# Projection and decode attention of a hybrid decoder step as one stage: keys turned in 32x32 blocks by VectorE, scores over four key quarters at once, one convolution operation per tap

## The chip, the cores and the metric

The kernel runs on one core of one Trainium2 chip. The metric is the device time of one execution in microseconds (us), as the median of several. "GB/s" is what the core's 16 DMA engines moved. PE is TensorE, PEld its weight load, DVE is VectorE, ACT is ScalarE, POOL is GpSimd, SP is SyncE, which here only issues DMAs.

## What is computed

One inference step with one layer: 256 prompt tokens and 8 sequences of 4 new tokens (32 decode tokens, 288 in all), model width 1024, all float32. Each token goes through a mixer with two head groups and then through a mixture of 32 experts. What matters here is the input projection, the short convolution of head group A, and the decode part of head group B, whose 8 sequences have 1024 past keys and values each, in pages of 128 rows that a page table scatters over a pool:

```python
proj = h @ w_in
qkv_g, z_g, beta_in, a_in, qkv_s = jnp.split(proj, [c1, c2, c3, c4], axis=-1)
conv_out, conv_new = causal_short_conv(qkv_g, conv_buf, conv_w)      # width 4, then SiLU
...
past_k = cache_k[l][page_table].reshape(bs, -1, SB_HEADS, HEAD_DIM)  # 8 heads x 64
z = jnp.einsum('bqhd,bkhd->bhqk', q_blk, k) * scale + bias_f
mask = key_pos[None, :] < pos[:, None]
log_rem = jnp.where(mask, jax.nn.log_sigmoid(-z), 0.0)
after = lax.cumsum(log_rem, axis=3, reverse=True) - log_rem
a = jnp.where(mask, jnp.exp(jax.nn.log_sigmoid(z) + after), 0.0)
out = jnp.einsum('bhqk,bkhd->bqhd', a.astype(v.dtype), v)
```

So each weight of a key is sigmoid(z) times the product of (1 - sigmoid(z)) over all later keys. Head group A (a delta rule in chunks of 64) and the experts follow; the change hardly touches them.

## The kernel before

The program is written by hand: each engine has its own list of instructions, in blocks, and semaphores (`wait_ge`, `then_inc`) tie the engines together. Every engine executes its list strictly in order. At the end of a block all engines meet. A ring of 12 slots of 1 MB (`ring`, `slot(u)`) holds whatever is loaded: the projection's weights in 7 column groups of 2 MB, then the cache pages, then `w_out`, and later the experts' chunks.

**Block 1, projection.** `tiles` is the order of the 29 output tiles of 128 columns: 12 `conv`, `ba`, 4 `z`, 4 `q`, 4 `k`, 4 `v`. For each tile PE does 8 matmuls of 128x128 by 128x288 (L410), ACT copies the result out, DVE does the convolution (`conv`, eight operations for each tile, L627 to L631: four taps, each once for the prompt and once for the decode tokens) and the multiplication by the sigmoid (`silu`, L639). After the next tile PE turns what must lie token by token (`turn`).

**Block 2, decode attention.** 16 steps (`STEPS`), each with one page of keys of 4 sequences. In a step PE turns the 16 key blocks by matmuls with the identity (`turn_keys`, L824), ACT and DVE copy half of them each out of PSUM (L947, L993), and PE forms the scores (`scores`, L836), with sequences side by side in four groups of 32 PE columns. For each half of 512 keys ACT makes two sigmoids (`betas`, L915), DVE a running product and a multiplication (`past_weights`, L973, L975), PE turns the weights (`turn_A`, L848), and `values` (L859) sums the value pages, which lie in the ring as loaded. `own_heads` (L872) picks each head's own columns. Pages are loaded by `load_cache`, one page at a time: a `value_load` of the page's number (L206) and then the DMA (L207), from SP and from GpSimd.

Then come block 3 (prompt part of head group B and first products of group A, up to 265.8 us), the rest of group A, `w_out`, the router and, from about 376 us on, the experts in 16 pairs. Their weights stream from HBM through the same ring (L761).

Of the kernel before, what the change touches and what calls it, by code (L numbers as in the profile page):

```python
# [13 lines left out]
ALU = mybir.AluOpType  # L14
# [7 lines left out]
NH = 8  # L22
# [38 lines left out]
def build(nc, x_prompt, x_sample, cache_k, cache_v, page_table, state_conv, state_ssm, norm_mix, w_in, conv_w,  # L61
# [4 lines left out]
    with ctx:  # L66
# [10 lines left out]
        X = sb("X", [P, 3, D])  # L77
        wb = sb("wb", [P, D])
# [42 lines left out]
        E = const(2, P)  # L121
        Sel = const(2, 16)
        headmask = const(512)
        sel8, hch = const(P), const(512)
# [12 lines left out]
        vs_tok, zg = at(A1, (3, GW)), at(A1 + 3 * GW, (HP, T))  # L137
# [6 lines left out]
        s_small, s_small2 = sem("conv_state_loaded"), sem("small_loaded")  # L144
# [5 lines left out]
        s_ringfree = sem("ring_used")  # L150
# [6 lines left out]
        s_ax, s_ex, s_qbd = sem("abs_a"), sem("log1p_a"), sem("query_blocks")  # L157
# [5 lines left out]
        GROUP_COL = [0, GW, 2 * GW, C_Z, C_S, C_S + GW, C_S + 2 * GW]  # L163
# [7 lines left out]
        s_gpage = [sem(f"pages_loaded_by_gpsimd{i}") for i in range(4)]  # L171
# [4 lines left out]
        def slot_count(u):  # L176

            return sum(16 * (PGL if U_C <= v < U_WO else 1) for v in range(u % NSLOT, u + 1, NSLOT)
                       if (U_C <= v < U_WO and v - U_C not in BY_POOL) or (not U_C <= v < U_WO and v % 2 == 0))

        def slot_wait(eng, u):
            m = u - U_C
            if U_C <= u < U_WO and m in BY_POOL:
                return eng.wait_ge(s_gpage[m % 8 // 2], PGL * 16 * ((m - 11) // 8 + 1))
            return eng.wait_ge(slot_sem(u), slot_count(u))

        def slot_free(eng, u, n):

            if u + n > NSLOT:
                eng.wait_ge(s_ringfree, u + n - NSLOT)  # L190

        def load_w_in(eng, n):
            slot_free(eng, 2 * n, 2)
            eng.dma_start(slot(2 * n, 2).rearrange("p (k n) -> p k n", k=KD),
                          w_in_v[:, :, GROUP_COL[n]:GROUP_COL[n] + GW]).then_inc(slot_sem(2 * n), 16)

        CACHE_UNITS = [("k", 0, 1), ("k", 0, 0), ("v", 0, 1), ("k", 1, 1), ("v", 0, 0), ("k", 1, 0), ("v", 1, 1), ("v", 1, 0)]

        def load_cache(eng, m):

            (what, g, ph), pg = CACHE_UNITS[m // 4], m % 4
            kv = "kv".index(what)
            slot_free(eng, U_C + m, 1)
            for s in range(4):
                col = NPG * (4 * g + s) + PGL * ph + pg
                page = eng.value_load(pt[0:1, col:col + 1], min_val=0, max_val=POOL - 1)  # L206
                eng.dma_start(slot(U_C + m)[:, s * GW:(s + 1) * GW],  # L207
                              (cache_k, cache_v)[kv][0, bass.ds(page, 1)].rearrange("o p h d -> (o p) (h d)"))\
                   .then_inc(s_gpage[m % 8 // 2] if m in BY_POOL else slot_sem(U_C + m), 16)
# [7 lines left out]
        class Norm:  # L217


            def __init__(self, nth, rowbuf, weight_wait, turned, ready=lambda e: None, inner=1):  # L220
                self.order = lambda v: v.rearrange("p (q k) -> p k q", k=inner)
                self.dest = lambda v: v.rearrange("p (k q) -> p k q", k=inner)
                self.rowbuf, self.weight_wait, self.turned, self.ready = rowbuf, weight_wait, turned, ready
                self.base = 3 * nth

            def scalar(self, act):
                self.ready(act)
                for t in range(3):
                    r = rows(t)
                    act.activation(self.rowbuf(t), X[r, t, :], ACT.Square, accum_out=stat[r, t, 0:1]).then_inc(s_nsq, 1)  # L230
                for t in range(3):
                    r = rows(t)
                    act.wait_ge(s_nsq, self.base + t + 1)
                    act.activation(stat[r, t, 1:2], stat[r, t, 0:1], ACT.Sqrt, scale=1.0 / D,
                                   bias=epst[r, 0:1]).then_inc(s_nstd, 1)
                if self.turned:
                    for t in range(3):
                        act.wait_ge(s_ntp, self.base + t + 1)
                        b = 2 * (t % 2)
                        n = ROWS[t]  # L240
                        act.activation(hT[:, :, toks(t)],
                                       bank[:, b:b + 2, :].rearrange("p b n -> p (b n)")[:, 0:KD * n]
                                       .rearrange("p (k n) -> p k n", k=KD), ACT.Copy).then_inc(s_nev, 1)

            def vector(self, dve):
                c = Chain(dve, s_dve)
                c.n = dve_n[0]
                self.weight_wait(dve)
                for t in range(3):
                    r = rows(t)  # L250
                    dve.wait_ge(s_nstd, self.base + t + 1)
                    c(dve.reciprocal(stat[r, t, 2:3], stat[r, t, 1:2]))
                    dve.scalar_tensor_tensor(out=self.dest(self.rowbuf(t)), in0=self.order(X[r, t, :]), scalar=stat[r, t, 2:3],
                                             in1=self.order(wb[r, :]), op0=ALU.mult, op1=ALU.mult).then_inc(s_nrow, 1)
                dve_n[0] = c.n

            def tensor(self, pe):
                for t in range(3):
                    pe.wait_ge(s_nrow, self.base + t + 1)
                    if t == 2:  # L260
                        pe.wait_ge(s_nev, self.base + 1)
                    b, n = 2 * (t % 2), ROWS[t]
                    dst = bank[:, b:b + 2, :].rearrange("p b n -> p (b n)")
                    for k in range(KD):
                        ins = pe.transpose(dst[:, k * n:(k + 1) * n], self.rowbuf(t)[:, k * P:(k + 1) * P],
                                           ident[0:n, 0:n])
                    ins.then_inc(s_ntp, 1)


        hrow = lambda t: work[rows(t), A2 + D * t:A2 + D * (t + 1)]  # L270
        s_id, s_t = sem("identity_ready"), sem("turned")

        B0 = A2
        pad = [work[:, B0 + 316 * i:B0 + 316 * i + 315] for i in range(2)]
        B1 = B0 + 632
        turnT = [work[:, B1 + T * i:B1 + T * (i + 1)] for i in range(2)]
        B2 = B1 + 2 * T
        csig = work[:, B2:B2 + 2 * T].rearrange("p (b n) -> p b n", b=2)
        B3 = B2 + 2 * T

        cdec, cpro = work[0:NSEQ * 7, B3:B3 + CONVD], work[64:67, B3:B3 + CONVD]
        kst = at(B3 + CONVD, (3, GW))
# [2154 lines left out]
```

## Time and profile before

| | |
|---|---|
| time, median of 3 | 1309.69 us (1308.79 to 1310.25) |
| span of the profiled execution | 1313.2 us, 20103 instructions |
| profiled execution against the median | 3.5 us above it |
| PE, DVE, ACT, POOL busy | 1253.0, 402.9, 247.9, 97.3 us |
| moved | 463.64 MB, mean 353 GB/s |

The page names no other time for the profiled execution than its span, first to last instruction. A stretch of one stage is read from the windows and from the time line, not from the shares over the whole span.

### The profile page before, as it was taken

The numbers are of one execution on the slowest core, as the hardware profiler recorded it, in microseconds if no ns is written. First come the engines' busy times: TensorE is split into PE (matmuls) and PEld (weight loads), VectorE is DVE, ScalarE is ACT, GpSimd is POOL, SyncE is SP. The second block draws the span as 40 slices with busy tenths as digits, with TensorE's granted clock in tenths as the row PEclk, the third lists the DMA queues.
The fourth block names the chain that finished last, engine by engine and source line by source line (L and its number), as shares of the span: only waits on it lengthen the run. The fifth ranks groups of instructions, "written<-read, shape, count | busy, mean of one in ns | idle before, by whom it ended". The sixth has DMA issues, their size and how long they took to land.

```text
span 1313.2 us, 20103 instructions
## 1 busy us (share of the span) xinstructions
PE 1253.0 (95%) x7924; PEld 566.2 (43%) x7924; DVE 402.9 (31%) x912; ACT 247.9 (19%) x416; POOL 97.3 (7%) x172
## 2 busy tenths in 40 slices
PE   8999998989999999999999999999999999999996
PEld 6777775687443333333333333333333333333332
DVE  4721343642742222322222232222213322212323
ACT  3223332623211110110111011011101101011103
POOL 6101142252000000000000000000000000000000
PEclk9999998999989999999999999999999999999999
DMA  9643699020799999999999999999999999999994
GB/s 319 237 128 92 226 373 339 9 88 7 280 334 382 425 428 429 426 429 428 428 430 425 429 428 424 431 428 429 425 430 429 426 430 426 430 427 427 429 427 185
DMA packets 68156, 463.64 MB, mean 353 GB/s; under 512 B 16910, under 2 KB 17038, under 8 KB 41478
## 3 DMA queue, kind: packets, MB, share of 16 engines
q1 hardware_dynamic: 64536, 451.17, 83.9%
q0 software_dynamic: 3520, 11.54, 2.4%
q8 instruction: 38, 0.62, 0.2%
q10 hardware_dynamic: 46, 0.18, 0.0%
q14 instruction: 16, 0.13, 0.0%
HBM read 459.15 MB, written 3.70 MB: 352 GB/s over the span
## 4 chain that ended last, share of the span: by engine, by line
PE 55%; DMA 23%; issue 1%; ACT 1%; DVE 0%; SPq 0%; DVEq 0%; ACTq 0%
PE bank L2130 25%; DMA ring<-in_w_up 20%; PE bank L2163 6%; PE bank L2099 4%; PE bank L2078 4%; PE bank L2143 3%; PE bank L1588 2%; DMA ring<-in_w_down 2%; PE bank L2082 1%; PE bank L2103 1%; PE bank L1453 1%; PE bank L1443 1%; PE bank L1450 1%; PE bank L2190 1%; PE bank L2119 0%
## 5 line engine op out<-in xcount | busy, mean ns | idle before, releaser
L2130 PE MATMUL bank<-ring,work 128*64 128x512 f32 x1280 | 288.5, 604 | 19.4 <-DMA ring<-in_w_up 19.4
L2130 PEld LDWEIGHTS bank<-ring,work 128*64 128x64 f32 x1280 | 91.7, 139 | 213.5 <-issue 202.9
L2163 PE MATMUL bank<-ring,work 128*64 128x512 f32 x768 | 172.3, 596 | 7.7 <-ACT work L2265 5.3
L410 PE MATMUL bank<-hoT,ring 128*128 128x288 f32 x448 | 115.1, 412 | 0.8 <-ACT hoT L445 0.5
L2163 PEld LDWEIGHTS bank<-ring,work 128*64 128x64 f32 x768 | 54.8, 137 | 103.4 <-issue 98.7
L410 PEld LDWEIGHTS bank<-hoT,ring 128*128 128x128 f32 x448 | 84.9, 193 | 23.7 <-issue 0.7
L2364 DVE TENSOR_SCALAR work<-bank 128x512 f32<-128x512 f32 x32 | 22.1, 690 | 231.5 <-PE bank L2143 230.5
L2249 ACT ACTIVATE work<-bank 128x1024 f32<-128x1024 f32 x16 | 16.4, 1024 | 385.9 <-PE bank L2082 365.1
L2323 DVE TENSOR_TENSOR X<-X,bank 128x512 f32<-128x512 f32 x64 | 44.0, 688 | 120.7 <-PE bank L2099 120.7
L2377 DVE COPY work<-bank 128x512 f32<-128x512 f32 x16 | 11.1, 692 | 211.5 <-PE bank L2163 211.5
L2099 PE MATMUL bank<-work 128*128 128x512 f32 x128 | 59.2, 605 | 0.0
L2143 PE MATMUL bank<-ring,work 128*64 128x512 f32 x256 | 56.3, 592 | 1.5 <-DMA ring<-in_w_up 1.5
L2130 PE MATMUL bank<-work 128*64 128x512 f32 x128 | 56.6, 595 | 0.0
L2130 PE MATMUL bank<-hoT,work 128*64 128x512 f32 x128 | 56.6, 595 | 0.0
L2143 PE MATMUL bank<-work 128*64 128x512 f32 x128 | 56.2, 592 | 0.0
L2163 PE MATMUL bank<-hoT,work 128*64 128x512 f32 x128 | 56.2, 592 | 0.0
L2143 PE MATMUL bank<-hoT,work 128*64 128x512 f32 x128 | 56.2, 592 | 0.0
L2163 PE MATMUL bank<-work 128*64 128x512 f32 x128 | 56.2, 592 | 0.0
L2078 PE MATMUL bank<-gq,work 128*128 128x512 f32 x120 | 54.0, 592 | 0.0
L2261 ACT ACTIVATE work<-work 128x512 f32<-128x512 f32 x32 | 20.1, 627 | 144.5 <-DVE work L2364 144.5
L2369 DVE TENSOR_TENSOR work<-work 128x512 f32<-128x512 f32 x32 | 38.9, 1215 | 18.8 <-ACT work L2261 16.6
L2265 ACT ACTIVATE work<-bank 128x512 f32<-128x512 f32 x32 | 19.1, 597 | 111.4 <-PE bank L2171 111.4
(414 smaller groups left out, 1396.2 us busy)
## 6 DMA issues: line engine op xcount, KB each, us to landing
ring<-in_w_up SPq DMA_DIRECT2D x96, 2048.0 KB, 24.7
ring<-in_w_down SPq DMA_DIRECT2D x48, 2048.0 KB, 26.6
work<-in_w_up SPq DMA_DIRECT2D x16, 2048.0 KB, 24.2
hoT<-in_w_up SPq DMA_DIRECT2D x16, 2048.0 KB, 28.6
work<-in_w_down SPq DMA_DIRECT2D x16, 1024.0 KB, 22.7
hoT<-in_w_down SPq DMA_DIRECT2D x16, 1024.0 KB, 24.6
ring<-in_w_in SPq DMA_DIRECT2D x7, 2048.0 KB, 16.0
ring<-in_cache_k SPq DMA_DIRECT2D x48, 256.0 KB, 3.0
```

Source lines behind the costliest of these rows:

```text
L410: ins = pe.matmul(bank[0:m, i % 2, 0:T], w[:, k, :], hT[:, k, :], start=k == 0, stop=k == KD - 1)
L1588: ins = pe.matmul(bank[q, WO_BANK[t, m], :], oT[:, k, toks(t)], w[:, k, :], start=k >= HP if t == 2 else k == HP, stop=k < HP if t == 2 el ...
L2078: pe.matmul(bank[:, 6 + m, :], Pm[:, t * P:(t + 1) * P], h2[:, t, 512 * m:512 * (m + 1)], start=t == 0, stop=False)
L2099: pe.matmul(bank[:, 4 + n, :], PGT[:, t * P:(t + 1) * P], oo[:, 512 * m:512 * (m + 1)], start=True, stop=True).then_inc(M["y"], 1)
L2130: ins = pe.matmul(bank[CAP * e:CAP * e + CAP, g, :], xT[:, k, CAP * e:CAP * e + CAP], weight(odd, ch + e, k % 2 * RSLOT + 512 * g), start= ...
L2143: ins = pe.matmul(bank[CAP * e:CAP * e + CAP, g, :], xT[:, k, CAP * e:CAP * e + CAP], weight(odd, 6 + e, k % 2 * RSLOT + 512 * g), start=F ...
L2163: ins = pe.matmul(bank[CAP * e:CAP * e + CAP, 4 + m, :], aT[:, k, CAP * e:CAP * e + CAP], weight(odd, ch + e, k % 4 * D + 512 * m), start= ...
L2261: act.activation(sg, gb, ACT.Sigmoid, scale=1.702).then_inc(M["sigmoid"], 1)
L2265: act.activation(aT[:, 4 * half:4 * half + 4, :].rearrange("p k s -> p (k s)"), bank[:, half, :], ACT.Copy)\
L2323: dve.tensor_tensor(x, x, bank[:, 4 + n, :], ALU.add).then_inc(M["y_added"], 1)
L2364: dve.tensor_scalar(gb, hu[:, :, 0], 7.0, None, ALU.min).then_inc(M["gate_clamped"], 1)
L2369: dve.tensor_tensor(ab[:, 512 * half:512 * (half + 1)].rearrange("p (k q) -> p k q", k=4), by_k(ub), by_k(sg), ALU.mult).then_inc(M["act"], 1)
```

## The change

Blocks 1 and 2 become one block. The attention's projections come first (`q`, `k`, `v`, `ba`, then `conv` and `z`), and pieces of the decode attention stand between the tiles on each engine's list. Nearly everything is loaded in 25 pairs of slots (`PAIRS`), 2 MB each, by SP alone, in the written order; pair n waits until pair n-6 has been used up. A pair of keys or values is now all 8 pages of one sequence. A page of keys goes to 32 partitions, four rows of the page side by side, so that eight pages fill the tile; VectorE turns it in place in 32x32 blocks (two instructions of 128x2048), after which one matmul contracts 32 dimensions of 4 key groups (a quarter of the keys each) at once with a block-diagonal query matrix `Q32`. `Q32` lies over `X` and `wb`, so x is loaded again later. The running product goes over 256 keys per group, and small operations join the four groups. The convolution runs over prompt and decode tokens in one operation per tap; GpSimd does the SiLU multiplication and the squares, VectorE the normalisation that GpSimd did. The gate of `z` moves into block 3 (one ACT and one DVE operation over 128x1152).

```diff
-        U_C, U_WO, U_END = 14, 46, 50
-        PGL = 4
-        BY_POOL = [m for m in range(11, 32) if m % 2]
+        PAIRS = [("w", "q"), ("K", 0), ("K", 1), ("w", "k"), ("K", 2), ("K", 3), ("w", "v"), ("V", 0), ("V", 1), ("K", 4), ("K", 5),
+                 ("w", "c0"), ("V", 2), ("V", 3), ("w", "c1"), ("K", 6), ("K", 7), ("w", "c2"), ("V", 4), ("V", 5), ("w", "z"),
+                 ("V", 6), ("V", 7), ("o", 0), ("o", 1)]
...
-            for s in range(4):
-                col = NPG * (4 * g + s) + PGL * ph + pg
-                page = eng.value_load(pt[0:1, col:col + 1], min_val=0, max_val=POOL - 1)
-                eng.dma_start(slot(U_C + m)[:, s * GW:(s + 1) * GW],
...
+                def used(q):
+
+                    what, n = PAIRS[q]
+                    if what == "w":
+                        sp.wait_ge(s_pj, group_end(n) + 1)
+                    elif what == "K":
+                        sp.wait_ge(s_sc, n + 1)
+                    else:
+                        sp.wait_ge(s_av, n + 1)
+
+                def load_pair(q):
+                    what, n = PAIRS[q]
+                    if what in "KV":
+                        order = KEY_PAGES if what == "K" else range(NPG)
+                        pages = [sp.value_load(pt[0:1, NPG * n + pg:NPG * n + pg + 1], min_val=0, max_val=POOL - 1) for pg in order]
+                    if q >= NPR:
+                        used(q - NPR)
...
+                    elif what == "K":
+                        for pg, page in zip(order, pages):
+                            kb, odd = pg // 2, pg % 2
+                            sp.dma_start(tile[32 * kb:32 * kb + 32, 4 * GW * odd:4 * GW * (odd + 1)].rearrange("p (q c) -> p q c", q=4),
...
+                load_x()
+                sp.dma_start(pt, page_table.rearrange("(o s) n -> o (s n)", o=1)).then_inc(s_pt, 16)
+                load_pair(0)
+                sp.wait_ge(s_pt, 16)
+                for q in range(1, len(PAIRS)):
+                    load_pair(q)
...
+                    for s in (2 * b, 2 * b + 1):
+                        pe.wait_ge(s_kt, s + 1)
+                        keys = pair_tile("K", s).rearrange("p (g c) -> p g c", g=8)
+                        for m in range(4):
+                            for j in range(HP):
+                                cb = 4 * j + m
+                                ins = pe.matmul(bank[32 * j:32 * j + 32, 6, 256 * (s % 2):256 * (s % 2) + 256]
...
+                    if i == 19:
+                        turn_A(2)
+                        own_heads(1)
+                        scores(3)
...
+                    if i == 22:
+                        turn_A(3)
+                        own_heads(2)
+                    if i == 24:
+                        values(3)
+                        square_sums(range(3))
+                    if i == 25:
+                        square_sums(range(3, 5))
...
+                def turn_keys(s):
+
+                    pair_wait(dve, "K", s)
+                    for h in range(2):
+                        v = pair_tile("K", s)[:, 2 * PAST * h:2 * PAST * (h + 1)]
+                        ins = dve.transpose(out=v, in_=v)
+                    ins.then_inc(s_kt, 1)
...
+                    if i == 18:
+                        own(1)
+                        turn_keys(6)
+                    if i == 19:
+                        turn_keys(7)
+                    if i == 21:
+                        own(2)
+                        weights(3)
```

**How the lists stand now, at three places.** SP, where the first cached keys are loaded. Before (`ring<-in_cache_k` is a page of keys into the ring, `TENSOR_LOAD` with its `ISA` rows the reading of one page number):

```order
L206 TENSOR_LOAD work [waits ring_used,small_loaded]
L206 ISA x2
L207 ISA
L207 DMA ring<-in_cache_k 128x512
L206 TENSOR_LOAD work
L206 ISA x2
L207 ISA
L207 DMA ring<-in_cache_k 128x512
```

Of the change, the last page number of the pair and the first pages of V0, the first pair that waits for the scores:

```order
L298 TENSOR_LOAD work
L298 ISA x2
L314 ISA [waits scores_done]
L314 DMA ring<-in_cache_v 128x512
L314 ISA
L314 DMA ring<-in_cache_v 128x512
```

A pair's eight page numbers are now read ahead of the pair's wait and its eight DMAs; they are as many as before for each page, and all of them are SP's.

VectorE, where the last two sequences' keys are turned (of the change; L916 and L918 are the convolution's taps, L906 is the multiplication by the head mask, L837 the turning):

```order
L916 TENSOR_SCALAR work<-work 128x312 [waits conv_silu,projection_copied]
L918 SCALAR_TENSOR_TENSOR work<-work 128x312 [waits dve_chain] x3
L906 TENSOR_TENSOR work<-bank,work 128x512 [waits heads_turned,values_summed]
L837 STREAM_TRANSPOSE ring<-ring 128x2048 [waits slot_loaded4]
L837 STREAM_TRANSPOSE ring<-ring 128x2048
L916 TENSOR_SCALAR work<-work 128x312 [waits conv_silu,projection_copied]
L918 SCALAR_TENSOR_TENSOR work<-work 128x312 [waits dve_chain] x3
L837 STREAM_TRANSPOSE ring<-ring 128x2048 [waits slot_loaded6]
L837 STREAM_TRANSPOSE ring<-ring 128x2048
```

Between the two pairs of turnings now stands one whole tile's convolution, and ahead of the first another one and the mask.

TensorE, near the end of the stage (of the change; L503 is a projection tile, L464 and L471 the values, L491 the sums of squares):

```order
L464 MATMUL bank<-work 32x512 [waits slot_loaded4,slot_loaded6,own_heads,A_copied]
L464 MATMUL bank<-work 32x512
L471 MATMUL bank<-ring,work 32x512 x16
L491 MATMUL bank<-work 128x288 [waits convstate_copied,squares]
L491 MATMUL bank<-work 128x288 [waits squares] x2
L503 MATMUL bank<-hoT,ring 128x288 [waits slot_loaded2,projection_copied]
L503 MATMUL bank<-hoT,ring 128x288 x7
L387 MATMUL bank<-ident,work 59x128 [waits convstate_copied,projection_copied]
L491 MATMUL bank<-work 128x288 [waits logs_and_roots,squares] x2
```

Before, the sums of squares stood between the `k` tiles, and the logarithms that the fourth one waits for (`logs_and_roots`, on ACT) were made tile by tile beside them; now the first logarithm stands on ACT's list behind the copy of tile 25.

## Rows read from the trace of the kernel before

**Rows 1.** Windows by stage: busy time of each engine, granted clock, DMA share, GB/s

```profile
0.00:145.80 145.80, 137.87 (x594) 101.99 (x595) 54.68 (x168) 39.71 (x105) 32.62 (x98) 1.00 0.58 188
145.80:220.20 74.40, 68.54 (x1014) 49.98 (x1014) 29.70 (x35) 25.66 (x33) 23.85 (x44) 1.00 0.99 359
376.00:1313.00 937.00, 898.86 (x4140) 311.28 (x4138) 240.26 (x527) 127.13 (x178) 0.00 (x0) 0.99 0.98 415
```

**Rows 2.** The chain that ended last, in time: start, us, what

```profile
681.01 7.07 PE bank L2130 x32
688.81 26.68 DMA ring<-in_w_up
...
748.76 25.49 DMA ring<-in_w_up
```

**Rows 3.** Time line of PE in block 1: start, us, what

```profile
14.96 10.13 PE L410 MATMUL bank<-hoT,ring 128*128 128x288 f32 x32 [0.47 <-ACT hoT L445]
...
130.66 0.49 PE L387 MATMUL bank<-ident,work 128*128 128x128 f32 x3
130.99 4.05 PE L410 MATMUL bank<-hoT,ring 128*128 128x288 f32 x16
134.87 0.49 PE L387 MATMUL bank<-ident,work 128*128 128x128 f32 x3
```

**Rows 4.** Time line of PE in block 2 and at its end

```profile
149.56 2.08 PE L824 MATMUL bank<-ident,ring 128*128 128x128 f32 x16 [0.33 <-ACT hoT L947]
151.57 1.08 PE L836 MATMUL bank<-hoT,work 128*32 128x128 f32 x32
...
173.43 3.62 PE L859 MATMUL bank<-ring,hoT 128*32 128x512 f32 x32
...
202.62 1.07 PE L872 MATMUL bank<-work,wb 128*128 128x16 f32 x8
...
212.10 1.92 PE L859 MATMUL bank<-ring,hoT 128*32 128x512 f32 x16 [3.31 <-DMA ring<-in_cache_v]
...
220.24 0.82 PE L1130 MATMUL bank<-work 64*64 64x65 f32 x16 [0.57 <-PEq L793]
```

**Rows 5.** Time line of SP, DMA issues: start, us, what

```profile
2.35 1.25 SPq L194 DMA_DIRECT2D ring<-in_w_in  x2
3.65 6.53 SPq L319 DMA_DIRECT2D work<-in_sb_bias  x1
...
13.93 0.38 SPq L326 DMA_DIRECT2D wba<-in_w_in  x1
...
126.95 8.06 SPq L207 DMA_DIRECT2D ring<-in_cache_v  x8
```

**Rows 6.** Lines L206 and L207 on SP: duration ns min/median/max, landing times

```profile
L206 SPq TENSOR_LOAD <-work x84: 262/268/851, 50.2 to 200.4; - x84
L207 SPq DMA_DIRECT2D ring<-in_cache_k x32: 333/338/388, 51.2 to 114.9; - x32
DMA to landing us min/median/max: 2.5/2.9/3.8
```

**Rows 7.** Windows 182 to 200 us: only cache pages are being loaded

```profile
182.00:200.00 18.00, 18.00 (x275) 13.06 (x268) 8.16 (x10) 5.89 (x8) 8.04 (x15) 1.00 1.04 388
```

**Rows 8.** DVE groups by shape up to 220 us: busy us, mean ns | idle before

```profile
L630 DVE SCALAR_TENSOR_TENSOR gq<-work,gq 128x256 f32<-128x256 f32 x36 | 17.4, 485 | 1.3
L993 DVE COPY work<-bank 128x1024 f32<-128x1024 f32 x8 | 9.8, 1224 | 20.4 <-PE bank L824 20.4
L973 DVE TENSOR_TENSOR_SCAN work<-work 128x512 f32<-128x512 f32 x4 | 5.1, 1282 | 3.2 <-ACT work L916 3.1
L675 DVE MEMSET work<- 128x1024 f32 x1 | 0.9, 912 | 0.2 <-issue 0.2
```

**Rows 9.** ACT groups by shape up to 220 us

```profile
L463 ACT ACTIVATE hoT<-bank,epst 128x288 f32<-128x288 f32 x8 | 3.8, 497 | 0.8 <-PE bank L423 0.6
L457 ACT ACT_TABLE_LOAD x1 | 1.3, 1283 | 0.0
```

**Rows 10.** Windows around two falls of the granted clock (the column before the DMA share)

```profile
218.00:220.00 2.00, 1.06 (x8) 0.97 (x8) 0.54 (x1) 0.22 (x1) 0.00 (x0) 1.00 1.05 383
222.00:230.00 8.00, 8.00 (x49) 4.88 (x45) 2.53 (x3) 2.97 (x4) 0.83 (x2) 0.50 0.85 186
270.00:274.00 4.00, 2.22 (x76) 2.13 (x72) 0.69 (x1) 1.20 (x3) 4.00 (x3) 1.00 0.99 417
274.00:278.00 4.00, 3.81 (x89) 3.81 (x90) 1.69 (x3) 0.00 (x0) 0.15 (x1) 0.66 0.17 54
```

**Rows 11.** Time line at the end of block 3

```profile
264.65 0.83 DVE L1285 TENSOR_TENSOR ring<-ring,work 128x256 f32<-128x256 f32 x1
```

More of the change, by code:

```diff
@@ L215, in build @@
             sem(f"norm_{n}") for n in ("squares", "std", "rows", "turned", "copied"))
[L217 to L267, printed above, removed]
@@ L270, in build @@
         hrow = lambda t: work[rows(t), A2 + D * t:A2 + D * (t + 1)]
         s_id, s_t = sem("identity_ready"), sem("turned")
+        PADW, CW = 316, 312
         B0 = A2
[L274 to L281, printed above, removed]
@@ L282, in build @@
[L282 to L286 removed]
+        pad = [work[:, B0 + PADW * i:B0 + PADW * i + 315] for i in range(2)]
+        B1 = B0 + 2 * PADW
+        cbuf = [work[:, B1 + CW * i:B1 + CW * (i + 1)] for i in range(2)]
+        B2 = B1 + 2 * CW
+        csig = [work[:, B2 + CW * i:B2 + CW * (i + 1)] for i in range(2)]
+        B3 = B2 + 2 * CW
+        NCS = 3 + 7 * NSEQ
@@ L287, in build @@
+        cst = work[0:NCS, B3:B3 + CONVD]
+        B4 = B3 + CONVD
+        baT = work[0:2 * NH, B4:B4 + TP]
+        B5 = B4 + TP
+        turnT = [work[:, B5 + T * i:B5 + T * (i + 1)] for i in range(2)]
+        kst = at(B5 + 2 * T, (3, GW))
+        l2 = at(B5, (KD, T))
+        B6 = B5 + 2 * T + 3 * GW + 192
+        assert KD * T <= 2 * T + 3 * GW + 192
         gq = sb("gq", [P, 12, TP])
-        baT = work[0:2 * NH, B3 + 2 * CONVD:B3 + 2 * CONVD + TP]
-        tiles = [("conv", j) for j in range(12)] + [("ba", 0)] + [("z", j) for j in range(4)] + \
-                [("q", j) for j in range(4)] + [("k", j) for j in range(4)] + [("v", j) for j in range(4)]
@@ L291, in build @@
-        I_BA, I_Q, I_SS = 12, 17, 18
+        tiles = [("q", j) for j in range(4)] + [("k", j) for j in range(4)] + [("v", j) for j in range(4)] + [("ba", 0)] + \
+                [("conv", j) for j in range(12)] + [("z", j) for j in range(4)]
+        I_K, I_BA, I_C, I_Z = 4, 12, 13, 25
         turned_tiles = [i for i, (kind, _) in enumerate(tiles) if kind in ("k", "v", "ba")]
@@ new lines, in build @@
+        AT = work[:, ZG:ZG + 512]
+        om = work[:, ZG + 2 * T:ZG + 2 * T + 512]
+        incl = work[:, B6:B6 + 514].rearrange("p (s c) -> p s c", s=2)
+        B7 = B6 + 514
+        AnT = work[0:ND, B7:B7 + NH * ND]
+        B8 = B7 + NH * ND
+        seg, segT, aft, aftT = (work[:, B8 + 32 * i:B8 + 32 * i + 32] for i in range(4))
+        B9 = B8 + 128
+        Tnew, carry, im16, Sel2, d4 = work[:, B9:B9 + 8], work[:, B9 + 8:B9 + 10], work[:, B9 + 10:B9 + 26], \
+            work[:, B9 + 26:B9 + 34], work[:, B9 + 34:B9 + 38]
@@ L448, in _, with query_blocks @@
                 c = Chain(act, s_act)
-                m = 0
+                def query_blocks(a):
+                    act.wait_ge(s_q32, 1)
+                    act.wait_ge(s_pje, 4)
+                    for db in range(2):
+                        r = HD * a + 32 * db
+                        src = qsT[r:r + 32, :, SEQ:T].rearrange("p h (s i) -> p h s i", i=NDEC)
+                        for kb in range(4):
+                            dst = Q32[32 * kb:32 * kb + 32].rearrange("p s (h a d) n -> p h a d s n", h=HP, a=2)
+                            ins = act.activation(dst[:, :, a, db, :, 16 * a + 4 * kb:16 * a + 4 * kb + 4], src, ACT.Copy)
+                    return ins
@@ L730, in _ @@
+                    if i == 21:
+                        own(2)
+                        weights(3)
+                    if i == 25:
+                        own(3)
+                        log_gates()
+                for n in range(4):
+                    dve.wait_ge(s_rt, 8 + n + 1)
+                    dve.tensor_tensor(gq[:, 2 * n:2 * n + 2, 0:T], gq[:, 2 * n:2 * n + 2, 0:T], l2[:, 2 * n:2 * n + 2, :], ALU.mult)
                 dve_n[0] = c.n
@@ L1230, in _ @@
                 betas(1)
+                act.activation(zs, zg, ACT.Sigmoid).then_inc(s_zs, 1)
                 copy_kv(0)
```

862 lines of the change are left out of this document (431 added, 431 removed).

## The prediction

> **What bounds the kernel now.** I read the windows by stage first. Up to 145.8 us PE is busy 137.9 of 145.8 us and DMA 0.58 of the time: the projection is bound by PE. From 145.8 to 220.2 PE has 68.5 of 74.4 us and DMA 0.99: both are nearly full, and PE's work there contains the turning of the keys. From 376 us on DMA has 0.98 at 415 GB/s and PE 899 of 937 us [rows 1]. The chain of waits tells which of these two sets the end: from 681 us on it goes through the landing of `w_up`, with 25.5 to 26.7 us at a step [rows 2]. The experts are a stream that begins when the mixer ends, so I take the end to move one to one with the moment when block 3 begins, now 220.24 us [rows 4]. DVE, ACT and POOL are far from full everywhere. The whole question is thus: when does PE finish the new stage?
>
> **PE's own work.** A tile took 134.87 - 130.99 = 3.88 us to the row behind it, and three turns put 130.99 - 130.66 = 0.33 ahead of it [rows 3]. 29 x 3.88 = 112.5; 8 `k`/`v` turns 2.6; `ba` and 12 conv turns 1.8; masks 0.8; 8 sums of squares of 288 columns, each an eighth of a tile, 3.9. Scores: an old step's 32 matmuls of 128 columns take 1.0 to 1.1 us with four groups side by side [rows 4]; now a sequence has 16 matmuls of 256 columns, again four side by side, which I put at 1.85, and 8 x 1.85 = 14.8. Values: 3.6 us for 32 of 512 columns [rows 4], now a little more for two sequences with the new tokens, 4.5; x 4 = 18. Turning of weights and `own_heads`, 1.0 each [rows 4], x 4 = 8; new tokens 0.8. Sum 163.2. PE begins at 14.96 [rows 3], so alone it would end at 178.2. What is gone is 16 times 2 us of key turning [rows 4] and the waits at the end of block 2, such as 3.31 us [rows 4]; that is the promise, 42 us.
>
> **SP.** Eight page issues take 8.06 us, so a page costs (8.06 - 0.34)/7 = 1.10 us of SP, number and DMA together [rows 5, 6]. I split it into 0.64 for the number, which now stands ahead of the pair's wait, and 0.46 for the DMA. 16 pairs are 141 us of one queue that GpSimd used to share. A pair needs 8.8 us of SP but 2.1 MB / 388 GB/s = 5.4 us of transfer [rows 7]. SP, not the bytes, paces the pages. From the page table's landing near 8.8 us: K0 to 17.7, seven small DMAs (0.4 to 0.6 each [rows 5]) to 21.8, K1 to 30.6, then `w` for `k`, which lands 5.4 + 2.9 [rows 6] + 0.7 (K1's last page) later, 40.1. K2, K3 to 48.6; `w` for `v` lands 58.1. V0 waits in SP's order for the scores of sequence 0 (54); V0, V1, K4, K5 go out to 85; `w` for c0 lands 94.0. V3 waits for the first values (107); c1 lands 119.8, just in time.
>
> **PE's waits by this time line.** (1) First `k` tile: ready at 14.96 + 4 x 3.88 + 0.8 = 31.3, weights at 40.1: 8.8 us. (2) First conv tile: ready at 86.9, weights 94.0: 7.1. (3) Scores of sequences 6 and 7. DVE does them in order: mask, two turnings, a convolution, two turnings. The ring's turning has no row. Nearest rows, per element of a partition: MEMSET 912/1024 = 0.89 ns, COPY 1.2, SCAN 2.5 [rows 8]; so 1.8 to 5.1 us for 2048. I take 2.2, near the copy, since it also reads and writes once; 4.4 a sequence. The four convolution operations over 312 columns are 4 x about 0.56 us, from 485 ns for 256 [rows 8]. The keys are then 2.0 and 4.8 us late: 6.8. (4) `turn_A(3)` waits for a convolution, the mask and `weights(3)`: 4.0. (5) The fourth sum of squares waits for the first logarithm, which stands behind ACT's copy of tile 25, a sigmoid, and two table loads of 1.28 us [rows 9]: 4.9. Sum 31.6 us, so PE ends at 209.8; copy, two last logarithms, one table load, four exponentials and DVE's product make block 3 begin at 212.7, against 220.2: -7.5.
>
> **What the rows don't price.** *Key pages into 32 partitions.* Every page row is of 128 partitions. Lower bound: their rate, 388 GB/s, 5.4 us a pair. Upper bound: half of it, 10.8 us, if a quarter of the partitions takes only half of the engines' rate. Up to 8.8 it mostly hides behind SP's issuing. At 10.8 K0 to K3 push `w` for `k` and `v` back: my sum over the time line gives +20, at 9.4 +10.7, at 7.5 +4.2. I take 7.5, since pages for four partition groups are in flight together: +4.2. The Trainium skill, "SBUF — State Buffer", section "Door 1: The DMA port swizzle", has 32 partitions reach 8 of 16 ports (189 GB/s where all reach 328), and "Can I just issue two DMAs to hit both halves?" says that two transfers to both halves gain little; by it the term would be the one at 10.8 and the sum 1329, and no row of before shows such a transfer.
>
> *The clock.* Where PE had idled half of 208.8 to 220.2, the granted clock fell from full to 0.50 (1.2 GHz) for 222 to 230, and about 2 us of idle at 272 gave 0.66 over the next four [rows 10]. Half of 3.4 us is 1.7; of 10 us, 5. Three shorter waits at 1.7 and two longer at 2.6 make 10; part is absorbed where PE waits for DVE or ACT next: +8. Bounds 0 and 15.
>
> *The gate in block 3.* DVE is last there, to 265.48 [rows 11], and gets one operation over 128x1152, 1.2 ns each [rows 8]: +1.3; ACT's stays under PE. *Entry of block 3*: it ran 8 us at half clock [rows 10]; the new stage's tail idles less: -2.5 of 4.
>
> **At nothing**, with their cover: DVE's convolution (12 x 2.3, less than before) and POOL's SiLU and square (under 2 us a tile of 3.88); the query blocks, 16 small ACT operations, under PE's tiles; POOL's clearing of 128x4096 (3.6 us by rows 8 on DVE, perhaps twice that on POOL) under 16 us of `q` tiles; loading x again, 1.2 MB, late in the stage, where DMA has room (0.58 in block 1 [rows 1]). With the cover gone each costs 1 to 4 us. ACT's copies stay under 1 us a tile: 497 ns is an activation of 288 [rows 9].
>
> **Sum:** -7.5 + 4.2 + 8 + 1.3 - 2.5 = +3.5 us. The profiled execution's span is 1313.2, 3.5 above the median of 1309.7; so the span becomes 1316.7 and the median 1313.2.
>
> **Rivals.** 0.2% is 2.6 us, about what this kernel's measurement can tell from no change.
> (a) *Faster by a few us*: pages land at full rate and PE's waits stay too short or too well absorbed to lower the clock. -7.5 + 0 + 2 + 1.3 - 2.5 = -6.7, 1303; down to 1296 if the first `k` tile's wait (8.8) goes too, by a cheaper page on SP. For: DMA has slack outside K0 to K3. Against: the two falls of the clock [rows 10]. 0.26.
> (b) *PE-bound as in block 1*: SP's page costs less when numbers are read back to back, turning is 1.8 us. PE ends near 185, block 3 begins near 188, 32 us earlier: 1309.7 - 32 + 1.3 = 1279. Against: 1.10 us on SP for each page [rows 5]. 0.06.
> (c) *Nothing measurable*: the terms above cancel; 1307 to 1312. 0.17.
> (d) *Slightly slower, my forecast*: 1312.3 to 1319. 0.25.
> (e) *Key pages at half rate*: 9.4 us a pair instead of 7.5 adds 10.7 - 4.2 = 6.5, 10.8 adds 16; near the middle +9 beyond the forecast, 1322, and 1329 at the end. It decides above about 9 us a pair, where transfer passes SP's 8.8. 0.18.
> (f) *DVE's turnings at the scan's price*, 2 x 5.1 us a sequence instead of 4.4: wait (3) grows by 5.8 for each of two sequences, less some 2 that the other waits then save, and K2 to K5 delay the `turned` copies behind them: +9.5, 1323. For: a 32x32 turning isn't a streaming copy. Against: only the upper row says so. 0.08.
>
> **From these:** faster 0.26 + 0.06 = 0.32, same 0.17, slower 0.51. The losses hold most, and the working gives 1313; the range of (d) alone is 1312 to 1319. The range has to hold (a), (c), (d), and most of (e) and (f): 1296 to 1327, which leaves out (b) and the far ends.
>
> **What the profile of after would show.** Block 3 begins at about 225 (212.7 + 4.2 + 8), against 220.24. SP: 8.8 us per page pair, no idle between K0 and K3. The first `k` tile begins near 40, the first conv tile near 96, each after idle of over 6 us, then granted clock 0.5 for some us. A STREAM_TRANSPOSE of 128x2048 takes 2.2 us. PE idles ahead of `scores(3)` and of the fourth sum of squares. The key pages' issue-to-landing tells (e): over 5 us where it was 2.9 [rows 6]. Behind each of these: if the k tile starts at 35, SP's page is cheaper (b); if DVE's turning is near 5 us, (f).
> What would make it wrong altogether: a wait that I haven't seen in the new order, since on SP, DVE and ACT every wait holds all that is queued behind it. SP's waits for V0 and V3 hold K4 and the conv weights; DVE's waits for a landing of keys hold the `turned` copies and convolutions, on which ACT's copies and PE's next tiles depend. Or the experts, if they don't follow the stage one to one: being DMA-bound they would, but a stage that ends with the first experts' weights less far ahead in the ring would give part of a gain back.

## The result and the profile after

The changed kernel takes 1331.26 us (median of 4, 1329.68 to 1331.52) against 1309.97 for the kernel before, measured beside it (1308.79 to 1313.65): the medians are 21.3 us apart, and the ratio over all their executions is 1.0153, 95% interval 1.0137 to 1.0169. It is slower by 1.5%; the prediction was 1313 us, range 1296 to 1327. The profiled execution has a span of 1329.8 us.

Block 3 begins at 244.9 us, 25 us later than before; the prediction had 225, 5 us later, and 42 us earlier was the promise if TensorE never waited. In what follows K0 and V0 are the keys and values of sequence 0, and c0, c1, c2 and z the column groups of `w_in` for the conv and `z` tiles, as in `PAIRS`. TensorE's time line in the new stage, all rows ahead of which it idled for over 2 us (they answer to [rows 3, 4]):

```profile
42.80 10.99 PE L503 MATMUL bank<-hoT,ring 128*128 128x288 f32 x32 [9.51 <-DMA ring<-in_w_in]
105.36 6.56 PE L503 MATMUL bank<-hoT,ring 128*128 128x288 f32 x16 [12.26 <-DMA ring<-in_w_in]
139.41 6.60 PE L503 MATMUL bank<-hoT,ring 128*128 128x288 f32 x16 [4.75 <-DMA ring<-in_w_in]
163.48 1.93 PE L439 MATMUL bank<-ring,Xw 128*32 128x256 f32 x32 [2.95 <-DVE ring L837]
169.81 3.64 PE L439 MATMUL bank<-ring,Xw 128*32 128x256 f32 x32 [4.39 <-DVE ring L837]
195.64 2.07 PE L449 MATMUL bank<-ident,hoT 128*128 128x128 f32 x8 [4.42 <-DVE hoT L898]
223.97 2.26 PE L491 MATMUL bank<-work 128*128 128x288 f32 x4 [4.81 <-ACT work L624]
244.90 0.68 PE L1165 MATMUL bank<-work 64*64 64x65 f32 x16 [2.54 <-PEq L281]
```

Seven waits, 43.1 us, each where the prediction had placed one except the third (c1); the eighth row is block 3's own beginning. Behind a wait the next work is slow: the first conv tile takes 6.56 us where one takes 4.05. The windows show the two things that go with it: the granted clock, and what DMA moves while keys (84 to 92, 144 to 152), values and `v` weights (60 to 68) or c0's weights (98 to 104) come, and DMA almost idle from 109 to 121:

```profile
14.60:244.90 230.30, 184.47 (x1022) 125.55 (x1023) 98.38 (x167) 43.21 (x123) 36.85 (x101) 0.88 0.76 230
...
60.00:68.00 8.00, 8.00 (x63) 5.79 (x56) 5.12 (x4) 1.93 (x3) 0.00 (x0) 1.00 1.05 386
84.00:92.00 8.00, 8.00 (x37) 4.48 (x36) 6.06 (x15) 0.65 (x2) 0.00 (x0) 1.00 1.03 241
109.00:121.00 12.00, 12.00 (x83) 6.78 (x85) 8.11 (x15) 3.39 (x11) 0.13 (x1) 0.95 0.05 18
144.00:152.00 8.00, 8.00 (x51) 3.55 (x50) 5.53 (x14) 1.02 (x5) 2.20 (x4) 0.97 1.07 241
98.00:104.00 6.00, 0.00 (x0) 0.00 (x0) 0.00 (x0) 0.00 (x0) 0.00 (x0) 0.50 1.05 396
```

With keys the DMA engines are as busy as with values (share 1.03 to 1.07), but move 241 GB/s instead of 386. From issue to landing a page of keys took 3.0 to 13.1 us, median 6.8: the prediction's sign for rival (e), over 5 us, is there. SP's time line:

```profile
25.82 3.87 SPq L310 DMA_DIRECT2D ring<-in_cache_k  x8
29.73 0.45 SPq L303 DMA_DIRECT2D ring<-in_w_in  x1
...
60.40 13.57 SPq L314 DMA_DIRECT2D ring<-in_cache_v  x16
78.59 12.86 SPq L310 DMA_DIRECT2D ring<-in_cache_k  x16
...
92.51 0.43 SPq L303 DMA_DIRECT2D ring<-in_w_in  x1
98.24 27.41 SPq L314 DMA_DIRECT2D ring<-in_cache_v  x16
...
127.48 1.12 SPq L303 DMA_DIRECT2D ring<-in_w_in  x1
```

V0 goes out at 60.4, c0's weights at 92.5, and V3 and c1 stand in SP's queue until the first values (121) have freed V0. The turning has its price on VectorE:

```profile
L837 DVE STREAM_TRANSPOSE ring<-ring 128x2048 f32<-128x2048 f32 x16 | 36.0, 2286 | 17.7 <-DMA ring<-in_cache_k 17.7
```

### The profile page after: what moved, and what is told of

Same layout as the page of the kernel before. It is cut to its first block, busy times and chain, and to the rows that moved or that the text cites. A ratio compares the mean times of both kernels' runs of the same rounds, so it can differ in the third digit from the quotient of the medians.

```text
span 1329.8 us, 18991 instructions
## 1 busy us (share of the span) xinstructions
PE 1233.0 (93%) x7378; PEld 538.1 (40%) x7378; DVE 424.8 (32%) x887; ACT 236.1 (18%) x417; POOL 87.2 (7%) x162
## 4 chain that ended last, share of the span: by engine, by line
PE 54%; DMA 22%; issue 1%; ACT 1%; DVE 0%; SPq 0%; DVEq 0%; ACTq 0%
PE bank L2169 25%; DMA ring<-in_w_up 20%; PE bank L2202 6%; PE bank L2138 4%; PE bank L2117 4%; PE bank L2182 3%; PE bank L1626 2%; DMA ring<-in_w_down 2%; PE bank L2121 1%; PE bank L2142 1%; PE bank L1481 1%; PE bank L1491 1%; PE bank L1488 1%; PE bank L2229 1%; PE bank L2158 0%
## 5 line engine op out<-in xcount | busy, mean ns | idle before, releaser
L503 PE MATMUL bank<-hoT,ring 128*128 128x288 f32 x448 | 127.6, 446 | 27.0 <-DMA ring<-in_w_in 26.5
L503 PEld LDWEIGHTS bank<-hoT,ring 128*128 128x128 f32 x448 | 92.6, 211 | 58.3 <-issue 30.5
L2362 DVE TENSOR_TENSOR Xw<-Xw,bank 128x512 f32<-128x512 f32 x64 | 44.0, 687 | 122.1 <-PE bank L2138 122.1
L2416 DVE COPY work<-bank 128x512 f32<-128x512 f32 x16 | 11.1, 692 | 211.6 <-PE bank L2202 211.6
L837 DVE STREAM_TRANSPOSE ring<-ring 128x2048 f32<-128x2048 f32 x16 | 36.0, 2286 | 17.7 <-DMA ring<-in_cache_k 17.7
```

The costliest lines, as they stand in the source:

```text
L503: ins = pe.matmul(bank[0:m, i % 2, 0:T], w[:, k, :], hT[:, k, :], start=k == 0, stop=k == KD - 1)
L837: ins = dve.transpose(out=v, in_=v)
L2362: dve.tensor_tensor(x, x, bank[:, 4 + n, :], ALU.add).then_inc(M["y_added"], 1)
```

## The experiments

All times are medians; "before" is the kernel before measured beside each run, 1309.6 to 1311.2 us. "Less" without more is against the changed kernel's 1331.26.

**A second trace of before.**

> The kernel before once more, for a second trace of it: the profiled execution of before took 3.5 us more than the median and lost it between 266 and 377 us, if that was a matter of this execution; then this trace has a span near 1309, block 3 again begins at 220.2, and the experts begin near 373 instead of 376.9. If the stretch is always that long, the experts begin at 377 again.

Measured: span 1308.0, block 3 at 219.38 (220.24 in the first trace), the experts at 371.95 (376.91). The first trace thus held 5.0 us that belonged to its execution, 3.4 of them behind 266 us. Compared with this one, the changed kernel's block 3 begins 25.5 us later; block 3 itself is 2.5 us shorter (42.4 against 44.9), the rest up to the experts 1.1, and the experts begin 22.0 later, at 393.91: which is the difference of the medians, 21.3, within 1 us. It lies in the new stage.

**Rate and issue of the pages.** Three kernels. In the first, keys lie over 128 partitions (the scores are then those of wrongly placed keys):

```diff
-    sp.dma_start(tile[32 * kb:32 * kb + 32, 4 * GW * odd:4 * GW * (odd + 1)]..., cache_k[...]"o (q r) h d -> (o r) q (h d)"...)
+    sp.dma_start(tile[:, GW * pg:GW * (pg + 1)], cache_k[...]"o p h d -> (o p) (h d)"...)
```

> Key pages are loaded as the value pages lie, each over 128 partitions; nothing else changes (the scores are then those of wrongly placed keys; the work is the same). Rate theory: what pushed the projection's weights back is that a page into 32 partitions moves at about 250 GB/s; then a pair of keys falls from 8.4 to 5.4 us, the waits of PE ahead of the first k tile (9.5 us) and the first conv tile (12.3 us) shrink by 4 to 8 us together, and the time by 15 or more below 1331. Issue theory: SP's 8.6 us for each pair of pages sets the pace whatever the transfer takes; then the GB/s of a pair rises, the waits stay within 2 us of what they were, and the time stays at 1329 to 1331. Both at once, by my sum over the time line: 1325, 6 us less, since the queue then waits for SP.

In the second the page numbers of keys and values are constants (other pages are attended to, and a pair's eight pages lie next to each other in memory):

```diff
-    pages = [sp.value_load(pt[0:1, NPG * n + pg:NPG * n + pg + 1], ...) for pg in order]
+    pages = [NPG * n + pg for pg in order]
```

> The page numbers are constants instead of being read from the page table: SP issues the same 128 page transfers without the 0.6 us for each number (other pages are attended to; the work is the same). Issue theory: SP's pair falls from 8.6 to 3.9 us, the two long waits of PE shrink by over 10 us together, the time to 1310 or less. Rate theory: keys still move at 250 GB/s, 8.4 us a pair, so the weights behind them come at most by the first pages' head start earlier, 4 us, and the time is 1325 or more. My sum for both at once: 1318.

> The two edits together. If rate and issue are two paces of the same stream, of which the slower sets the time, each alone brings little and both together much more than their sum: my sum gives 1300, 31 us less than 1331, against 19 for the two alone. If only one of them matters, the result is that of the one.

Measured: 1326.03, 1327.26 and 1305.94 us, so 5.2, 4.0 and 25.3 us less; the third has ratio 0.9971 (0.9955 to 0.9987) to before. Neither theory alone holds: rate and issue are two paces of one stream, and mending one leaves the other. My sums for that had 1325, 1318 and 1300: right for the first, 9 and 6 us too low for the others. The third shows what both paces are worth together, not that the kernel before was free of them: numbers at no cost relieve the values too, and before had to read its numbers as well. TensorE's waits ahead of the `k` and the first conv tile were 9.4 and 10.8 us in the first kernel, 7.6 and 7.9 in the second, and in the third:

```profile
32.68 9.69 PE L502 MATMUL bank<-hoT,ring 128*128 128x288 f32 x32 [1.24 <-DMA ring<-in_w_in]
112.12 5.65 PE L502 MATMUL bank<-hoT,ring 128*128 128x288 f32 x16 [3.25 <-DMA ring<-in_w_in]
...
215.70 0.68 PE L1164 MATMUL bank<-work 64*64 64x65 f32 x16 [2.54 <-PEq L281]
```

The wait ahead of the first conv tile is gone; the one at 112 is c1's.

**Why keys are slow.** A block ahead of the stage loads pages in eight forms and does nothing else (one execution):

> A block ahead of the stage loads 16 pages of keys of 256 KB (12 in the last form) in eight forms, one form after the other, and does nothing else, so that each form has its own stretch of some 11 us or more: (1) each page over 128 partitions, one row of 2 KB each; (2) 32 partitions with four rows each, groups in the kernel's order, neighbours far apart; (3) the same in the order of the pages; (4) as (2), every second page from ACT's queue; (5) 64 partitions from 0, two rows each; (6) 64 partitions from 32; (7) as (1) from two queues; (8) 32 partitions, always the first group. Partition theory: what counts is how many of the partitions a page covers, not the 2 KB rows, which are the same in all: forms 1 and 7 move 380 GB/s or more, 2, 3 and 8 about 250; form 6, in both halves, is well above form 5. Queue theory: pages of two queues run at once, so form 4 gets above 330. If the partitions don't matter and the changed kernel's 250 GB/s come from its pace of issue, forms 2 and 3 move 350 or more.

Windows inside the forms, in their order (the last column is GB/s):

```profile
8.00:12.00 4.00, 0.00 (x0) 0.00 (x0) 0.00 (x0) 0.00 (x0) 0.00 (x0) 1.00 1.02 387
20.00:32.00 12.00, 0.00 (x0) 0.00 (x0) 0.00 (x0) 0.00 (x0) 0.00 (x0) 1.00 1.07 236
38.00:54.00 16.00, 0.00 (x0) 0.00 (x0) 0.00 (x0) 0.00 (x0) 0.00 (x0) 1.00 1.07 213
64.00:70.00 6.00, 0.00 (x0) 0.00 (x0) 0.00 (x0) 0.00 (x0) 0.00 (x0) 1.00 1.06 352
76.00:92.00 16.00, 0.00 (x0) 0.00 (x0) 0.00 (x0) 0.00 (x0) 0.00 (x0) 1.00 1.07 200
102.00:108.00 6.00, 0.00 (x0) 0.00 (x0) 0.00 (x0) 0.00 (x0) 0.00 (x0) 1.00 0.94 337
114.00:122.00 8.00, 0.00 (x0) 0.00 (x0) 0.00 (x0) 0.00 (x0) 0.00 (x0) 1.00 1.05 394
126.00:138.00 12.00, 0.00 (x0) 0.00 (x0) 0.00 (x0) 0.00 (x0) 0.00 (x0) 1.00 1.07 201
```

The same 2 KB rows move at 387 GB/s over 128 partitions, 236 into groups of 32 that alternate between the halves, 213 in the order of the pages, 201 into one group. 64 partitions that lie in one half give 200, 64 across the middle 337. So it is the half of the partitions that is reached at one moment, not the 32. The half and the 64 that are no better than 32 agree with the Trainium skill, "SBUF — State Buffer", section "Door 1: The DMA port swizzle". Two queues, each in its own half, give 352: 49% above one queue. The same page of the Trainium skill gives, in the section "Can I just issue two DMAs to hit both halves?", two transfers to both halves 6%; for these page streams the measurement decides.

**TensorE's clock.** Matmuls that nobody reads, ahead of the seven waits:

```diff
+    for _ in range(n):
+        pe.matmul(bank[:, 2, 0:256], ident[:], hT[:, 0, 0:256], start=True, stop=True)
```

> Ahead of each of the seven long waits TensorE now does matmuls of 128x256 whose result nobody reads, each block sized a little shorter than the wait; nothing else changes. Clock theory: of the 25 us by which block 3 begins later, about 16 are work at half clock behind the waits (the k tiles, the first tile of c0 and of c1, the turning of the last weights, the last sums of squares), and a wait for a landing comes earlier when PE is earlier, since SP's order hangs on PE's progress; then the granted clock of the stage rises from 0.89 to about 0.97 and the time falls by 10 to 14, to 1317 to 1321. Rival: what runs at half clock is absorbed by the next wait, and the time stays at 1328 or more.

Measured: 1322.22, 9.0 us less; granted clock of the stage 0.99 (to 234.5 us) instead of 0.88, block 3 at 234.55. The `k` weights still land at 43.8, and two waits for weights (1.4 and 4.4 us) stay. But 9.0 is the least that the clock is worth: c0's weights landed at 104.8 (issued at 91.2, 13.6 us to landing) while the filling ran until 108.5, and c1's at 139.2 while it ran until 140.4. The filling itself so cost up to 3.6 and 1.2 us, and the clock is worth 9 to 14 us.

**Order of the loads, and places of the work.**

```diff
-  PAIRS = q K0 K1 k K2 K3 v  V0 V1 K4 K5 c0 V2 V3 c1 K6 K7 c2 V4 V5 z  V6 V7 o0 o1
+  PAIRS = q k  K0 K1 K2 v K3 V0 K4 V1 c0 K5 V2 V3 c1 K6 K7 V4 c2 V5 V6 V7 z  o0 o1
```

> Only the order of the 25 pairs on SP changes: the weights for k come ahead of the first keys, those for v and c0 each one or two pairs earlier, and z's last. Order theory: the bytes and SP's time for each pair are the same, but PE's first two long waits (9.5 and 12.3 us) and that ahead of c1 (4.8 us) go, with the half clock behind them, while the waits for DVE and ACT (22 us ahead of the last scores, the last weights and the fourth sum of squares) stay: my sum gives 23 us less, 1308. Supply theory: SP and DMA are full through the stage whatever the order, so the wait only moves to a later pair, and the time is 1325 or more.

Measured: 1323.74, 7.5 us less, a third of what I had worked out. The `k` wait is gone, but c0 is waited for 5.2 us, c1 4.2 and `v` 2.4, and 4.7 us go where TensorE waits for VectorE's copy, which stands behind the turning of K3.

```diff
-  turn_keys(6) after tile 18, turn_keys(7) after 19, weights(3) after 21 behind own(2); square_sums(3, 4) after 25, (5 to 7) after 26
+  turn_keys(6) after tile 17, turn_keys(7) after 18, weights(3) after 20;               square_sums(3, 4) after 26, (5 to 7) after 27
```

> Only the places on the lists of VectorE and TensorE change: the last two turnings of keys come one tile earlier, the last weights ahead of a convolution and of the mask, and the last five sums of squares one tile later, behind tiles 26 and 27. Place theory: the waits of 2.95, 4.39, 4.42 and 4.81 us and most of the half clock behind them go, while the waits for loads stay: my sum gives 12 us less, 1319. Rival: the same work only collides elsewhere on VectorE, whose mask for the second pair of sequences then comes later, and the time stays within 3 us of 1331.

Measured: 1323.14, 8.1 us less (12 expected); the five executions spread from 1317.9 to 1326.4. Four waits of 16.6 us in sum became three, 1.5 for the last keys, 3.2 for values and 1.5 for VectorE's mask. But in the traced execution, the slowest of the five, `k` was waited for 14.0 us and c1 6.0.

> Both edits, the order of the pairs and the places of work. If PE's waits are the whole loss, the two gains add up: 35 us less than 1331, so 1296, block 3 begins near 210, 14 us faster than the kernel before. If the supply of pages sets the stage once PE waits less, it comes out at 1305 or more, near the better of the two alone.

Measured: 1310.42, ratio 0.9996 (0.9982 to 1.0010): 20.8 us less than the changed kernel, and as fast as before, not faster. The two alone sum to 15.6; the difference is of the size of their spread. 35 was expected: in the trace the loads set a part again (waits of 4.3, 6.2 and 5.0 us for weights).

> Order and places as in the run before, and key pages over 128 partitions (the scores are of wrongly placed keys; the work is the same). Supply theory: after the order is mended, what is left of PE's waits (4.3, 6.2 and 5.0 us for weights, 2.8 for values) comes from the keys' 250 GB/s; then they go, and the time falls from 1310 by 12 or more, to 1298 or less. Issue theory: SP's page numbers hold it; then it falls by less than 5.

Measured: 1299.84, ratio 0.9920 (0.9894 to 0.9946): 10.6 us less, between the two theories. The waits for c0 (5.2) and c1 (4.2) stay; the rate is not all that makes them.

> Order and places as in the run before, and matmuls that nobody reads ahead of the three waits for weights and of the last scores. The half clock behind these waits costs some 8 us by my sum over the tiles; with the clock kept the time falls by 4 to 7 from 1310, to 1303 to 1306, and the kernel is faster than before. If the waits for loads take the gain back, it stays at 1309 or more.

Measured: 1312.78, ratio 1.0013 (0.9995 to 1.0030): a miss. In its trace TensorE waits 4.5 us for VectorE's copy (3.4 without the filling) and 4.4 for values (2.8), and block 3 begins at 222.1 where it began at 223.2: c0's weights landed at 97.3 as without the filling (97.2), c1's at 129.7 (131.2). What the filling gives back ahead of such a landing goes into the wait for it.

**Keys from two queues.** `KEY_PAGES[::2]` (partitions 0 to 63) from SP, `KEY_PAGES[1::2]` from ScalarE, two pages at a time between its copies.

> The changed kernel's order and places, and nothing left out: of each pair of keys SP issues only the four pages for the partitions 0 to 63, ScalarE's queue the four for 64 to 127 (two at a time between its copies). In the run on page forms two queues on opposite halves moved about 350 GB/s, one queue 238. If rate and issue of the key pages are the cause, both are relieved at once (6.0 instead of 8.4 us of transfer, 4.4 instead of 8.6 us of SP for a pair), and the time falls to 1308 to 1316, towards the 1306 of the run with both edits. If ScalarE's 1.1 us for each page holds its copies and with them TensorE (35 us more on its list), the gain is lost there and the time is 1325 or more.

> The same division of the key pages together with the order of pairs and the places of work of the run that had both; nothing is left out. Keys over all partitions gave 1300 there against 1310; two queues relieve SP too, so I expect 1294 to 1302, and the kernel faster than before by about 1%. If ScalarE's list becomes the wait, it stays at 1308 or more.

Measured: 1340.34, ratio 1.0208 (1.0180 to 1.0237), 9 us more than the changed kernel; and 1312.95, ratio 1.0007 (0.9982 to 1.0031). Both forecasts missed, and the first not as its rival said: ScalarE's copies were not held, TensorE idles for weights as before (`k` 14.4 us, c1 10.2). The `k` weights went out at 21.0, 8.7 us earlier than in the changed kernel, but took 25.2 us to land instead of 12.9; pages that the two queues issued behind them, at 24 to 27 us, landed at 34 to 40, ahead of them. So the weights shared the DMA engines with later pages, and the window 30 to 45 moved 268 GB/s. ScalarE's pages also go out when its list allows, not beside SP's: four pages of K3 stood behind the copy of the first `k` tile until 55 to 58 us. Which of the two costs how much isn't shown. GpSimd's queue was not tried.

**One late release.** The first values, and ScalarE's copy for them, come after tile 12 instead of 14:

```diff
                     if i == 12:
                         turn_A(0)
+                        values(0)
                     if i == 14:
-                        values(0)
                         scores(2)
```

> In the changed kernel only the first values move: TensorE sums them, and ScalarE copies their weights, two tiles earlier, ahead of the first conv tile, where TensorE waits 12.3 us for weights. V0 and V1 landed there long before. Release theory: SP's V3 and behind it c1 wait for these values (98 to 121 us, DMA idle from 109 to 121), so that the one late release also makes the 4.8 us wait ahead of c1; then 4.6 us of work go into the wait, c1's wait and its half clock (2.5 us) go, and the time falls by 9 to 13, to 1318 to 1322. If SP's order isn't held by it, only the 4.6 us come back, 1326 or more.

> The same move together with the order of pairs and the places of work, nothing left out. There c0 is waited for 6.2 us and c1 5.0, with DMA idle from 106 to 116 us. Release theory: both waits go but for 1 to 2 us, and the time falls from 1310 to 1296 to 1301, which is faster than the kernel before by 0.7 to 1.1%. If the keys' rate takes it back (the later pairs land as late as they did), it stays at 1306 or more.

Measured: 1322.09 (9.2 us less than the changed kernel, ratio to before 1.0108, 1.0065 to 1.0151, so uncertain by some 6 us; in its trace c1's wait is gone, c0's is 2.9 us instead of 12.3, and `k` is waited for 11.1), and 1305.05, ratio 0.9967 (0.9949 to 0.9985): with order and places the interleaved kernel is faster than before by 0.33%. In the trace of the latter DMA's idle window has gone (106 to 116 us: share 0.99; in the run without the move 0.20), and TensorE waits so:

```profile
55.93 5.81 PE L503 MATMUL bank<-hoT,ring 128*128 128x288 f32 x16 [3.90 <-DMA ring<-in_w_in]
69.61 0.53 PE L403 MATMUL bank<-ident,work 128*128 128x128 f32 x3 [3.10 <-DVE work L941]
122.34 6.92 PE L503 MATMUL bank<-hoT,ring 128*128 128x288 f32 x16 [4.45 <-DMA ring<-in_w_in]
...
212.46 0.68 PE L1167 MATMUL bank<-work 64*64 64x65 f32 x16 [1.96 <-PEq L281]
```

c0's wait is gone; c1 is still waited for, since K4 to V3 ahead of it now fill the stream (14.6 to 212.4 us: DMA share 0.92, where the changed kernel had 0.76). That gain is 5.4 us of the 9 to 14 expected.

## Why the prediction was wrong

The direction held, and so did the kind of loss: TensorE waits, and the half clock behind the waits. The size didn't, and one step of the mechanism failed: how a late event in SP's order comes back to it. Block 3 begins at 244.9 instead of 225. Term by term, to that point:

- **PE's own work**, 163.2 us: by the time line 14.61 to 242.36, less 43.1 idle, 16.8 of half clock (below) and 1.8 by which the first four tiles were slow, 166.1. 3 us too low. Scores (3.64 for two sequences) and values (4.7) were right. The first two tiles were as slow before (10.13 us [rows 3]); I had not counted it.
- **Waits**, 31.6 + 4.2: 43.1. `k` 8.8 against 9.5; first conv tile 7.1 against 12.3; last keys 6.8 against 7.3; weights 4.0 against 4.4; squares 4.9 against 4.8; c1 nothing against 4.75. The four that I had counted from VectorE's and ScalarE's lists were right in sum within 0.9 us, 15.7 against 16.6 (the keys singly were 2.95 and 4.39, not 2.0 and 4.8), with the turning at 2.286 us where I took 2.2. Wrong was the size in the step "Key pages into 32 partitions. [...] I take 7.5": 241 GB/s are 8.7 us a pair. By the prediction's own points (+4.2 at 7.5, +10.7 at 9.4) that is some 4 us more, so the rate doesn't carry the miss alone. The step that failed is the time line of SP. "V0 waits in SP's order for the scores of sequence 0 (54)": it went at 60.4, since the `k` weights landed at 42.6 instead of 40.1 and the half clock behind that wait had put the scores back. c0's weights thus went out at 92.5 instead of 85 and took 12.8 us behind slow keys instead of 9.0. "c1 lands 119.8, just in time" has the same fault: V3 was held until 121 instead of 107, c1's weights went out at 127.5 and landed at 139.4. I had shifted a late event once and not let it run round the loop SP, DMA, VectorE, TensorE, SP.
- **The clock**, +8: 16.8 us, by the rows behind each wait less the same work at full clock (`k` 3.0, c0 2.5, c1 2.5, the last keys 2.7, the last weights 3.3, the last squares 2.8). Six waits were followed by it, where I had counted three short and two long ones; for the long ones I took 2.6 us without a working, and they cost 3.0 and 2.5. (The 3.4 and 10 us that I halved are how long the two falls of [rows 10] lasted.) That part of it "is absorbed" is borne out: filling the waits gave 9.0 us back, 13.8 at most. So the term was 1 to 6 us too low in what it costs, less than the rows behind the waits suggest; the waits hold the larger part of the miss.
- **Block 3 and its entry**, +1.3 - 2.5 = -1.2: -2.5. The gate is last on VectorE and takes 1.41 us; the entry gave 3.8, since the first 8 us of block 3 ran at granted clock 1.00 where they had run at 0.50 (219.4 to 227.4 us in the second trace of before). The experts followed the stage one to one.

A slip without weight: rival (a)'s lower end, 1303 less a wait of 8.8, is 1294 and not 1296.

Rival (e), key pages at half rate, named the place; its 1322 to 1329 stops short of 1331, and its threshold, "decides above about 9 us a pair, where transfer passes SP's 8.8", doesn't hold: at 8.7 us the two paces are equal, and just there neither can be mended alone (5.2 and 4.0 us singly, 25.3 together). Against rival (b) stood SP's 1.10 us for each page, which the trace bears out (12.86 us for 16 pages' DMAs with eight numbers between), but numbers at no cost bring 4 us alone.

Shown is: rate and issue together 25 us; order 7.5, places 8.1, first values 9.2 us, each alone; all three 26 us, no byte or operation less. That a delay runs round the loop is shown at V3, where moving the first values took c1's wait away; for V0 it is read from the time line. Open is how much of c1's last wait is rate and how much order, what GpSimd's help with the issue, which the kernel before had, is worth, and what two queues give when both halves go out in step.

## What to carry to other kernels

Where a queue in order feeds two kinds of work, list for each late load what it waits for and who issues the thing ahead of it, and run a delay through that loop more than once before pricing it. When a transfer and its issue have nearly the same pace, an experiment on one of them alone shows almost nothing, so change both in a third run. Move a consumer that frees buffers into a wait ahead of it before touching anything else: it cost nothing here and gave 9 us, give or take 6.

## What the runs showed of the hardware

- 256 KB pages move at 200 to 236 GB/s when each transfer reaches one half of the partitions and at 337 to 394 when each reaches both; 32 or 64 partitions within a half are the same (201 and 200). The DMA share is full either way (1.07 at 200 GB/s, 1.02 at 387), so only GB/s beside it tells the two apart.
- One queue that alternates between the halves gets 236, two queues in opposite halves 352.
- The turning of 128x2048 in 32x32 blocks takes 2.256 to 2.312 us in place, 1.1 ns for an element of a partition, near a copy.
- After 9.5 us of idle TensorE's granted clock was 0.50 (1.2 GHz) from 42 to 48 us; after 2.95 us at 163.48 the scores ran at full speed (1.93 us for 32 of 128x256), after 4.42 us the turning of the weights took 2.07 us where it takes 1.06.
- The stage's first matmuls ran at half pace (9 from 14.6 to 18.6 us, 18 in each 4 us after), though the granted clock of the profile stands at 1.00 there; no run shows why.
- With ScalarE's queue beside SP's, 2 MB of weights took 25.2 us to land, and pages issued after them landed first.
